# Second layer norm applied by ScalarE and GpSimd, and half of each layer norm's statistics taken earlier

## What is computed

```python
def layer_norm(x, g, b):
    mu = jnp.mean(x, axis=-1, keepdims=True)
    var = jnp.mean(jnp.square(x - mu), axis=-1, keepdims=True)
    return (x - mu) * lax.rsqrt(var + LN_EPS) * g + b

x = layer_norm(DEEPNORM_ALPHA * x + mix, ln1_g[l], ln1_b[l])
x = layer_norm(DEEPNORM_ALPHA * x + sq_relu_mlp(x, w_up[l], w_down[l]), ln2_g[l], ln2_b[l])
...
h = rms_norm(x, norm_g)          # x * rsqrt(mean(x^2) + RMS_EPS) * g, second block
u = h @ w_in
```

## Time and profile before

| | us |
|---|---|
| median of three executions | 1682.12 |
| profiled execution | 1681.69 |
| its span in the trace | 1679.9 |
| TensorE busy | 1562.6 |
| VectorE busy | 872.6 |
| ScalarE busy | 821.3 |
| GpSimd busy | 55.5 |

### The profile page before, as it was taken

One profiled execution on the slowest core, in us unless ns is written; L12 is line 12 of the kernel. 1 busy time (PEld: TensorE's weight loads), 2 busy tenths in 40 slices (PEclk: granted clock), 3 DMA queues, 4 the chain that ended last, 5 costly groups with the idle time before them and its releaser, 6 DMA issues.

```text
span 1679.9 us, 24257 instructions
## 1 busy us (share of the span) xinstructions
PE 1562.6 (93%) x9844; PEld 987.1 (59%) x9844; DVE 872.6 (52%) x1749; ACT 821.3 (49%) x1239; POOL 55.5 (3%) x133
## 2 busy tenths in 40 slices
PE   5999999998998999999967989899989998899997
PEld 2444485654485466666854636464765744566676
DVE  6723437876536665555573233354356233677732
ACT  4553567776214654545424445364045553577731
POOL 0000000000000000000000000001000000000000
PEclk8999999999999999999988999999999999799999
DMA  5332331111413433333352456301114322000001
GB/s 173 100 101 91 105 102 54 51 51 51 164 62 104 166 101 101 101 101 101 101 76 38 78 89 98 101 1 29 51 50 150 122 85 101 13 2 2 2 26 50
DMA packets 127118, 132.09 MB, mean 79 GB/s; under 512 B 9664, under 2 KB 124096, under 8 KB 126880
## 3 DMA queue, kind: packets, MB, share of 16 engines
q1 hardware_dynamic: 124240, 119.66, 25.7%
q0 software_dynamic: 2768, 10.89, 1.8%
HBM read 128.44 MB, written 2.10 MB: 78 GB/s over the span
## 4 chain that ended last, share of the span: by engine, by line
PE 63%; DVE 5%; DMA 3%; ACT 3%; issue 2%; POOL 0%; ACTq 0%; DVEq 0%
PE bank L589 7%; PE bank L590 7%; PE bank L591 7%; PE bank L632 7%; PE bank L628 4%; PE bank L630 4%; PE bank L629 4%; PE bank L782 3%; PE bank L798 3%; PE bank L772 3%; PE bank L647 2%; DMA wring<-in_even_w_in 2%; PE bank L766 2%; PE bank L834 1%; DVE wring L1602 1%
## 5 line engine op out<-in xcount | busy, mean ns | idle before, releaser
L589 PE MATMUL bank<-xT,whigh 128*128 128x512 f16 (+1 forms) x984 | 375.9, 382 | 21.6 <-DVE wring L1602 20.9
L590 PE MATMUL bank<-xT,whigh 128*128 128x512 f16 (+1 forms) x984 | 375.7, 382 | 0.0
L591 PE MATMUL bank<-xT,wring 128*128 128x512 f16 (+1 forms) x984 | 375.4, 381 | 0.0
L1602 DVE SCALAR_TENSOR_TENSOR wring<-wring,wsc,whigh 128x2048 f16<-128x2048 f32 (+2 forms) x96 | 221.8, 2310 | 159.7 <-ACT whigh L1115 159.4
L1133 ACT ACTIVATE whigh<-wring 128x2048 bf16<-128x2048 f32 (+2 forms) x96 | 180.2, 1877 | 224.2 <-DMA wring<-in_w_up 62.9
L1115 ACT ACTIVATE whigh<-wring,wsc 128x2048 f16<-128x2048 f32 (+2 forms) x96 | 189.2, 1971 | 120.1 <-DVE wsc L1552 101.5
L589 PEld LDWEIGHTS bank<-xT,whigh 128*128 128x128 f16 (+1 forms) x984 | 96.6, 98 | 141.2 <-issue 21.8
L591 PEld LDWEIGHTS bank<-xT,wring 128*128 128x128 f16 (+1 forms) x984 | 96.8, 98 | 118.1 <-issue 3.3
L590 PEld LDWEIGHTS bank<-xT,whigh 128*128 128x128 f16 (+1 forms) x984 | 96.7, 98 | 117.7 <-issue 5.4
L628 PE MATMUL bank<-whigh,slab 128*128 128x256 f16 x512 | 139.9, 273 | 2.9 <-DVE wring L1602 2.9
L630 PE MATMUL bank<-whigh,slab 128*128 128x256 f16 x512 | 139.9, 273 | 0.0
(11 more groups left out here) (273 smaller groups left out, 2296.9 us busy)
## 6 DMA issues: line engine op xcount, KB each, us to landing
wring<-in_w_in SPq DMA_DIRECT2D x28, 1024.0 KB, 5.0
wring<-in_w_up SPq DMA_DIRECT2D x16, 1024.0 KB, 5.3
wring<-in_w_down SPq DMA_DIRECT2D x16, 1024.0 KB, 5.1
wring<-in_even_w_in SPq DMA_DIRECT2D x16, 1024.0 KB, 9.6
wring<-in_odd_w_in SPq DMA_DIRECT2D x14, 1024.0 KB, 5.0
wring<-in_w_a SPq DMA_DIRECT2D x4, 1024.0 KB, 5.1
wring<-in_w_out SPq DMA_DIRECT2D x4, 1024.0 KB, 5.3
wring<-in_even_w_out SPq DMA_DIRECT2D x4, 1024.0 KB, 5.2
```

The costliest lines, as they stand in the source:

```text
L589: pe.matmul(bank, wh[:, k, wcol:wcol + width], xh[:, k, :], start=k == 0, stop=False)
L590: pe.matmul(bank, wh[:, k, wcol:wcol + width], xl[:, k, :], start=False, stop=False)
L591: mm = pe.matmul(bank, wl[:, k, wcol:wcol + width], xh[:, k, :], start=False, stop=k == KC - 1)
L1602: dve.scalar_tensor_tensor(low_of(i)[:, :, 0:m], wring[:, i % NSLOT, :, 0:m], wsc[:, n:n + 1], whigh[:, n % NHIGH, :, 0:m], ALU.mult, ALU. ...
```

## The change

For the second layer norm (`dn3`, the only stage with a layer norm and an RMS norm) the two VectorE passes are replaced. VectorE keeps the statistics and makes the inverse root and, new, -mean * inverse (`inverse_root`). ScalarE applies both in one Identity activation, x * inverse + (-mean * inverse), in place. GpSimd multiplies by the gain and then adds the offset (`second_norm`), both in place, with a semaphore between. ScalarE squares block t - 1 behind the centring of block t; the RMS norm of block t - 1 and the low half of block t - 2 follow on VectorE. In GpSimd's list block 0 stands ahead of the all-reduce of `qf` slot 0, and blocks 1 to 3 ahead of that of `qf` slot 1.

For both layer norms the bn_stats of columns 0 to 511 move: they are taken for each block when slot 1 has been added (`first_stats`), one block late, and for block 3 behind the low half of the stage's last slot. Only columns 512 to 1023 and the aggregate stay in the loop (`statistics`). The first layer norm is otherwise as before.

```diff
--- before.py
+++ after.py
@@ -509,6 +509,17 @@
                 pool.dma_start(dst, src.to_broadcast([P, DM]).rearrange("p (a n) -> p a n", a=2)).then_inc(s_(name + "_gain"), 16)
 
 
+            def second_norm(t):
+
+                x = res[:, t, :].rearrange("p (a n) -> p a n", a=2)
+                if t == 0:
+                    pool.wait_ge(s_("ln2_gain"), 16)
+                    pool.wait_ge(s_("ln2_b_gain"), 16)
+                pool.wait_ge(s_("ln2_centred"), t + 1)
+                pool.tensor_tensor(x, x, gain["ln2"][0], ALU.mult).then_inc(s_("ln2_scaled"), 1)
+                pool.wait_ge(s_("ln2_scaled"), t + 1)
+                pool.tensor_tensor(x, x, gain["ln2_b"][0], ALU.add).then_inc(s_("ln2_y"), 1)
+
             pool.wait_ge(s_("x_max"), 1)
             pool.partition_all_reduce(xexp[:, 0:1], xmax[:, 0:1], P, RMAX).then_inc(s_("x_all"), 1)
             for n in range(NSPLIT):
@@ -548,6 +559,11 @@
                             pool.dma_start(petab[i][HD * o:HD * o + HD, :],
                                            a[f"odd_pe_{x}_2"][0].rearrange("(k l) d -> l d k", l=2)[o],
                                            allow_slow_non_contiguous=True).then_inc(s_("nsa_in"), 16)
+                if n == split_index("qf"):
+                    second_norm(0)
+                if n == split_index("qf", 1):
+                    for t in range(1, TT):
+                        second_norm(t)
                 pool.wait_ge(s_("w_max"), n + 1)
                 pool.partition_all_reduce(wexp[:, n:n + 1], wsc[:, n:n + 1], P, RMAX).then_inc(s_("w_all"), 1)
             pool.wait_ge(s_("ct_mm"), 16)
@@ -1072,17 +1088,29 @@
                 if key:
                     size_of(slot_at(key, 0))
                 for t in range(TT):
-                    if ln and t >= lag:
-                        turned(rms or ln, banks, t - lag)
+                    if ln and not rms and t >= lag:
+                        turned(ln, banks, t - lag)
                     if key and t == 2:
                         high(slot_at(key, 0))
                     if ln:
                         root(ln, "ln", t)
-                    if rms:
-                        squares(rms, t, x or ln + "_y")
+                    if ln and rms:
+                        act.wait_ge(s_(ln + "_inv"), t + 1)
+                        act.activation(res[:, t, :], res[:, t, :], ACT.Identity, bias=stat[:, t, 18:19],
+                                       scale=stat[:, t, 16:17]).then_inc(s_(ln + "_centred"), 1)
+                    if ln and rms and t >= 1:
+                        squares(rms, t - 1, ln + "_y")
+                        root(rms, "rms", t - 1)
+                        if t >= lag:
+                            turned(rms, banks, t - lag)
+                    if rms and not ln:
+                        squares(rms, t, x)
                         root(rms, "rms", t)
                     if not ln and banks and t >= lag:
                         turned(rms, banks, t - lag)
+                if ln and rms:
+                    squares(rms, TT - 1, ln + "_y")
+                    root(rms, "rms", TT - 1)
                 if banks:
                     size_of(slot_at(key, 1) if key != "kc" else slot_at("vc", 0))
                     for t in range(TT - lag, TT):
@@ -1624,14 +1652,26 @@
             def folded(x):
                 return x.rearrange("p (a n) -> p a n", a=2)
 
-            def layer_norm(name, t):
-
-                x = folded(res[:, t, :])
-                for i in range(2):
-                    ins = dve.bn_stats(stat[:, t, 6 * i:6 * i + 6], res[:, t, i * 512:(i + 1) * 512])
-                ins.then_inc(dve_chain, 1)
+            def first_stats(name, t):
+                dve.wait_ge(s_(name + "_ev"), n_(name + "_ev", TT + t + 1))
+                dve.bn_stats(stat[:, t, 0:6], res[:, t, 0:512])
+
+            def statistics(name, t):
+
+                dve.bn_stats(stat[:, t, 6:12], res[:, t, 512:DM]).then_inc(dve_chain, 1)
                 dve.wait_ge(dve_chain, own(dve_chain))
                 dve.bn_aggr(stat[:, t, 15:17], stat[:, t, 0:12]).then_inc(s_(name + "_v"), 1)
+
+            def inverse_root(name, t):
+                dve.wait_ge(s_(name + "_r"), t + 1)
+                dve.reciprocal(stat[:, t, 16:17], stat[:, t, 16:17]).then_inc(dve_chain, 1)
+                dve.wait_ge(dve_chain, own(dve_chain))
+                dve.tensor_scalar(stat[:, t, 18:19], stat[:, t, 15:16], stat[:, t, 16:17], -1.0, ALU.mult, ALU.mult).then_inc(s_(name + "_inv"), 1)
+
+            def layer_norm(name, t):
+
+                x = folded(res[:, t, :])
+                statistics(name, t)
                 dve.wait_ge(s_(name + "_v"), t + 1)
                 dve.scalar_tensor_tensor(x, x, stat[:, t, 15:16], gain[name][0], ALU.subtract, ALU.mult).then_inc(dve_chain, 1)
                 return own(dve_chain)
@@ -1703,20 +1743,28 @@
                         add(name, 4 * s + t, s, t, banks, alpha)
                         if t == 1:
                             after(name, s)
+                        if ln and s == 1 and t >= 1:
+                            first_stats(name, t - 1)
                 low(slot_at(name, 3))
+                if ln:
+                    first_stats(name, TT - 1)
                 for g in ([ln, ln + "_b"] if ln else []) + ([rms] if rms else []):
                     dve.wait_ge(s_(g + "_gain"), 16)
                 for t in range(TT):
                     for s in (2, 3):
                         add(name, 8 + 2 * t + s - 2, s, t, banks, alpha)
                     dve.wait_ge(s_(name + "_ev"), n_(name + "_ev", 10 + 2 * t))
-                    if ln:
-                        if rms and t >= 1:
+                    if ln and rms:
+                        statistics(ln, t)
+                        inverse_root(ln, t)
+                        if t >= 1:
                             rms_norm(rms, dst, t - 1)
+                        if t >= 2:
+                            turned_low(rms, nbanks, t - 2)
+                    elif ln:
                         scaled = layer_norm(ln, t)
-                        lag = 2 if rms else 1
-                        if t >= lag:
-                            turned_low(rms or ln, nbanks, t - lag)
+                        if t >= 1:
+                            turned_low(ln, nbanks, t - 1)
                         layer_norm_end(ln, t, scaled)
                     else:
                         dve.sem_inc(s_(name + "_x"), 1)
```

More of the change, by code:

```diff
@@ L1625, in folded @@
                 return x.rearrange("p (a n) -> p a n", a=2)
+            def first_stats(name, t):
[4 more added lines that the diff above has]
+                dve.wait_ge(dve_chain, own(dve_chain))
+                dve.bn_aggr(stat[:, t, 15:17], stat[:, t, 0:12]).then_inc(s_(name + "_v"), 1)
+            def inverse_root(name, t):
+                dve.wait_ge(s_(name + "_r"), t + 1)
+                dve.reciprocal(stat[:, t, 16:17], stat[:, t, 16:17]).then_inc(dve_chain, 1)
+                dve.wait_ge(dve_chain, own(dve_chain))
+                dve.tensor_scalar(stat[:, t, 18:19], stat[:, t, 15:16], stat[:, t, 16:17], -1.0, ALU.mult, ALU.mult).then_inc(s_(name + "_inv"), 1)
             def layer_norm(name, t):
                 x = folded(res[:, t, :])
-                for i in range(2):
-                    ins = dve.bn_stats(stat[:, t, 6 * i:6 * i + 6], res[:, t, i * 512:(i + 1) * 512])
-                ins.then_inc(dve_chain, 1)
-                dve.wait_ge(dve_chain, own(dve_chain))
-                dve.bn_aggr(stat[:, t, 15:17], stat[:, t, 0:12]).then_inc(s_(name + "_v"), 1)
+                statistics(name, t)
                 dve.wait_ge(s_(name + "_v"), t + 1)
```

## The result

The changed kernel takes 1690.81 us (median of four executions, 1689.94 to 1694.41) against 1681.49 us before (a fourth execution has joined the three): 9.3 us more. The ratio of the means is 1.0061 with a 95% interval of 1.0037 to 1.0084, which is 10.2 us. That lies inside the range (forecast 1688.0, range 1680 to 1697), but most of the loss came by a way that the forecast had put at nothing.

What follows compares the result with a forecast made beforehand. VectorE, with ScalarE in its loop, was taken to bound the second layer norm, where TensorE waits. Second norm +7.4 and first norm -1.2 made +6.2 us on 1681.69; forecast 1688.0 us, range 1680 to 1697.

Steps and rivals of the forecast that it cites:

- Place, start and tail: Second norm's four-block loop: starts behind ScalarE's late weight slot; from block 3's squares to TensorE's restart a fixed 5.48 us.
- Early statistics: First columns' statistics behind slot 1: -1.2 us in the first norm; in dn3 TensorE starts slot 2 1.55 us later, free.
- the walk: Block-by-block schedule of the second norm with exclusive doors: squares of block 3 start at 892.5, +7.4 us.
- T: Duration of one GpSimd elementwise pass over 128x1024 f32, taken as 2.57 us, between 1.28 and 3.85.
- Centring: ScalarE's added pass per block in the second norm, taken as 1.06 us, like the squares.
- Doors: Second norm: two-input VectorE operations and GpSimd passes exclude each other, each waiting for the other's end; 4.8 us.
- the four collisions: Second norm: four waits between VectorE operations and GpSimd passes, 4.8 of the 7.4 us; without them +2.6.
- what it adds: Second norm, in series per block: two small VectorE operations (0.4 us), a ScalarE pass (1.06), two GpSimd passes (2.57 each).
- rival 4: GpSimd pays a reload when changing between all-reduce and elementwise work: one 6 us wait gives 1694; chance 0.05.
- rival 3: GpSimd passes in the second norm take 3.85 us, doors exclusive: +15 us, 1697; chance 0.10.
- same: Outcome for the whole kernel: change within the 5.05 us taken as measurable; chance 0.48.
- slower: Outcome for the whole kernel: time from 1687.2 us up; chance 0.46.

Runs made afterwards that it cites:

- no_reduce: The changed kernel with the all-reduces of qf slots 0 and 1 replaced by one-column GpSimd adds, which leaves out part of the work: 1684.2 us, ratio 1.0015.
- passes_on_vector: The changed kernel with gain and offset as two VectorE operations per block behind ScalarE's centring, GpSimd doing only all-reduces: 1682.4 us, ratio 1.0005.
- behind_reduce: The changed kernel with block 0's two GpSimd passes moved behind the all-reduce of qf slot 0: 1690.7 us, repeated at 1689.2 us.

## Why the prediction was right or wrong

**Place, start and tail: right.** The loop started right behind the late slot (root of block 0 at 854.76), and the tail stayed 5.48 us.

**Early statistics: right.** o1 gave 1.2 us (term: -1.2). In dn3 TensorE's wait for the last slot grew from 2.91 to 4.30, by 1.39 for the 1.55 forecast, and cost nothing. That they would give 1.7 us in dn3 too was not a term of its own, since the walk replaced the whole loop.

**T: near.** 2.35 us, between my 2.57 and the 2.25 that I had estimated from the Trainium skill, GPSIMD Engine Reference, section 3.1. It hides where the walk hid it. **Centring: mis-sized.** 1.24 us, not the 1.06 of the squares: 0.2 us a block.

**Doors: right in kind, priced too high.** The rows show both directions. VectorE's rms_norm took 1.65, 1.91 and (no_reduce) 1.80 us beside a pass and 1.28 without; the low half 3.12 for 2.35; GpSimd's offset 3.21 for 2.34 when it found VectorE at work. The ends tell how: the three rms_norm end 1.08 us behind the end of GpSimd's factor, the low half 2.15 us behind the end of GpSimd's offset, and the last offset 2.21 us behind the end of rms_norm. Each did nearly all of its work when the other was through. VectorE's line 1647, with one input from PSUM, ran inside a pass and kept its 1.40. This agrees with the exclusive lock of the Trainium skill, SBUF — State Buffer, section "Who interferes with whom". In my walk the four collisions made 4.8 us. The loop that has the walk's conditions, no_reduce, took 32.7 us, not the walk's 35.4, and its four on the path are 0.52, 0.64, 0.77 and 0.87: 2.8 us. On the changed kernel's path there were three (0.37 for rms_norm of block 1, 0.77 for the low half, 0.87 for the last offset): 2.0 us. These are sums of rows and no experiment.

**The step that failed: "what it adds".** I listed the passes and the semaphores between them, and took GpSimd's list as free to alternate. It alternates at 5.8 and 7.2 us, four times, of which one is hidden and the two behind block 0 are waited for: the scale of `qf` slot 0 came 3.2 us late for VectorE, and block 1's factor, whose input had been ready since 859.3, began at 875.10. That was rival 4, to which I gave 0.05. I said that rows gave it no price, and named one wait of 6 us from the Trainium skill; by the loops it is 42.4 - 32.7 = 9.7 us.

The whole, by loops: 28.0, - 1.7 (statistics), + 4.6 (through ScalarE), + 1.8 (GpSimd's passes and collisions in place of VectorE's), + 9.7 (reloads) = 42.4. My sum had +7.4 for a loop that grew by 14.4. That the time came near the forecast is luck: the range was wide upward for rival 3, which did not occur, and the executions showed 9.3 us where loop and o1 make 13.2. That it came out clearly slower is luck as well. I had given "same" 0.48 and "slower" 0.46, and what the forecast described, the move without reloads, is no_reduce: 2.0 us over before, less than the 5.05 us that I took for measurable.

**The 13 us of VectorE work that left the loop** bought nothing: VectorE waited instead, 17.7 us for ScalarE's RMS root (second row of the waits).

**Open.** Why both measurements (means +10.2 and +10.9) are below the 13.2 of loop and o1 can't be told beyond the spread, into which 13.2 fits: the intervals reach to 14.1 and 13.8. Whether a loop without collisions would be faster than passes_on_vector was not tried.

## What to carry to other kernels

An engine that looks idle can have a fixed price for changing the kind of its work, here 5.8 and 7.2 us: before moving a step to GpSimd, look at what kinds stand next to it in its list, and what waits behind each change. A step taken off the busiest engine of a serial loop pays only if the loop gets shorter; two more engines in series lengthened it: the way through ScalarE alone by 4.6 us, with nearly the same work on VectorE. And ask first what starts the loop: taking the first root ahead of one wait on ScalarE's list shortened the kernel, and moving work to two other engines lengthened it.

## What the runs showed of the hardware

GpSimd's changes of kind: 6.8 to 7.7 us from an all-reduce to a tensor_tensor, 5.75 to 6.0 us back, shown as "issue", also when the pass has one column, and hidden when GpSimd idles anyway. A pair of MODIFY_POOL_CONFIG stands in the trace at every one of them and, behind the program's start, nowhere else. A tensor_tensor of 128x1024 f32 takes 2.35 us on GpSimd and 1.23 on VectorE. The Identity activation with scale and bias per row takes 1.24 us on 128x1024 f32, Square 1.06. Executions of the kernel before spread over 7.6 and 11.3 us here, while a loop repeated within 0.3 us: 42.4 and 42.2 for the changed kernel, 37.9 and 38.1 for behind_reduce.
